# High parts first in grouped products, decay products moved ahead, in a two-block language model kernel

## The reference, cut to what matters

```python
# block 1, once a layer
h = rms_norm(x, norm1_g[l]) * (1 + sc1) + sh1
p = h @ w_in[l]
...
state = (state * w_t[:, :, None, :] - sk[..., None] * (a_t * kk_t)[:, :, None, :]
         + v_t[..., None] * k_t[:, :, None, :])            # one step of the recurrence
...
h2 = rms_norm(x, norm2_g[l]) * (1 + sc2) + sh2
x = x + gt2 * ((silu(gate) * up) @ w_down[l])
# block 2, once a layer
u = rms_norm_2(h, g_mix_pre)
gq, gk, gv, gg, ra_f, ra_b, ... = split(u @ w_in)
la_f = log_sigmoid(ra_f @ w_alpha_up[0] + b_alpha[0]) / 16   # decays of the four heads, and la_b
q_dec = q * exp(cum); k_intra = k * exp(-cum)                # cum: running sum of la in a chunk
...
h = h + rms_norm_2((silu(gate) * up) @ w_ffn_out, g_ffn_post)
h = h + rms_norm_2(sigmoid(h @ w_ple_gate) * e, g_ple_post)
```

## Time and profile before

| what | value |
|---|---|
| median of 3 runs | 3910.09 us (3908.43 to 3912.69) |
| profiled execution | 3911.07 us |
| its span, first to last instruction | 3909.2 us |
| TensorE, VectorE, ScalarE, GpSimd busy | 95%, 46%, 22%, 58% |
| mean granted TensorE clock | 0.975 |
| TensorE's share of the chain that ended last | 86% |
| weight chunks | 1082 of 256 KB |

### The profile page before, as it was taken

The page is one execution under the profiler, slowest core; times in us unless marked ns, Lnnn a source line. Parts: engine busy times, 40 slices in busy tenths (PEclk is TensorE's granted clock), DMA queues, the critical chain, the costliest instruction groups (busy, mean ns, idle before and its releaser), DMA issues.

```text
span 3909.2 us, 52952 instructions
## 1 busy us (share of the span) xinstructions
PE 3731.4 (95%) x21300; PEld 3022.7 (77%) x21300; DVE 1806.1 (46%) x2338; ACT 851.7 (22%) x1334; POOL 2274.0 (58%) x2218
## 2 busy tenths in 40 slices
PE   5999999999999899999899999999989999999997
PEld 4777678887777678887788677888777876778886
DVE  5643754234744653124443654523454435553235
ACT  3322110004222110003321532000243225220002
POOL 4512768776512767774556356777645463567773
PEclk9999999999999999998999999999989999999999
DMA  4223444342223443332223133333312231323332
GB/s 184 87 83 103 138 143 146 113 151 77 75 82 99 137 146 108 97 97 66 75 73 122 52 102 82 97 97 96 98 50 79 86 103 55 110 82 97 97 97 68
DMA packets 192195, 386.08 MB, mean 99 GB/s; under 512 B 21456, under 2 KB 21584, under 8 KB 190288
## 3 DMA queue, kind: packets, MB, share of 16 engines
q1 hardware_dynamic: 169776, 338.24, 29.1%
q10 hardware_dynamic: 22176, 44.45, 3.2%
HBM read 361.64 MB, written 20.97 MB: 98 GB/s over the span
## 4 chain that ended last, share of the span: by engine, by line
PE 86%; DVE 8%; ACT 4%; DMA 1%; issue 1%; ACTq 0%; SPq 0%; DVEq 0%
PE psum L420 18%; PE psum L421 18%; PE psum L422 18%; PE psum L492 3%; PE psum L494 3%; PE psum L493 3%; PE psum L514 2%; PE psum L981 1%; PE psum L956 1%; PE psum L599 1%; PE psum L611 1%; PE psum L467 1%; PE psum L468 1%; PE psum L469 1%; PE psum L618 1%; PE psum L572 1%
## 5 line engine op out<-in xcount | busy, mean ns | idle before, releaser
L2245 POOL TENSOR_SCALAR w_hi<-raw 128x512 fp32r<-128x512 f32 x1082 | 747.3, 691 | 1493.2 <-DMA raw<-weight_chunks 1489.5
L2247 POOL TENSOR_TENSOR w_lo<-raw,w_hi 128x512 fp32r<-128x512 f32 x1082 | 1491.1, 1378 | 90.3
L420 PE MATMUL psum<-in_hi,w_hi 128*128 128x512 f32 x1920 | 761.6, 397 | 3.8 <-ACT hs L1325 1.3
L421 PE MATMUL psum<-in_lo,w_hi 128*128 128x512 f32 x1920 | 749.3, 390 | 0.0
L422 PE MATMUL psum<-in_hi,w_lo 128*128 128x512 f32 x1920 | 748.8, 390 | 0.0
L420 PEld LDWEIGHTS psum<-in_hi,w_hi 128*128 128x128 f32 x1920 | 361.8, 188 | 91.7 <-issue 11.1
L421 PEld LDWEIGHTS psum<-in_lo,w_hi 128*128 128x128 f32 x1920 | 361.7, 188 | 79.8 <-issue 6.2
L422 PEld LDWEIGHTS psum<-in_hi,w_lo 128*128 128x128 f32 x1920 | 361.6, 188 | 75.7
L492 PE MATMUL psum<-in_hi,w_hi 128*128 128x512 f32 x576 | 255.0, 443 | 0.0
L494 PE MATMUL psum<-in_hi,w_lo 128*128 128x512 f32 x576 | 226.5, 393 | 0.0
L493 PE MATMUL psum<-in_lo,w_hi 128*128 128x512 f32 x576 | 226.4, 393 | 0.0
(11 more groups left out here) (427 smaller groups left out, 6700.4 us busy)
## 6 DMA issues: line engine op xcount, KB each, us to landing
raw<-weight_chunks SPq DMA_DIRECT2D x1082, 256.0 KB, 2.6
ada_col<-ada_slabs SPq DMA_DIRECT2D x80, 512.0 KB, 4.3
spill<-gate_st ACTq DMA_DIRECT2D x56, 256.0 KB, 2.7
ada_at<-ada_slabs SPq DMA_DIRECT2D x8, 1024.0 KB, 15.6
gin<-spill ACTq DMA_DIRECT2D x32, 256.0 KB, 3.4
mgs<-spill ACTq DMA_DIRECT2D x32, 256.0 KB, 3.0
sml<-small ACTq DMA_DIRECT2D x4, 1024.0 KB, 5.2
spill<-nt ACTq DMA_DIRECT2D x16, 256.0 KB, 2.6
```

The source lines that it names most:

```text
L420: pe.matmul(bank[:], wh, hi[:, i, :], start=(i == 0), stop=False)
L421: pe.matmul(bank[:], wh, lo[:, i, :], start=False, stop=False)
L2245: ts(w_hi[:, slot, :], raw[:, slot, :], 1.0, 1.0, ALU.mult, ALU.mult).then_inc(sem("chunk_hi"), 1)
L2247: ins = tt(w_lo[:, slot, :], raw[:, slot, :], w_hi[:, slot, :].bitcast(F32), ALU.subtract)
```

## The change

1. `late_group` and `group` become one function, `stepped`. For each tile it waits for `hi_ready`, issues for every member the two matmuls with the high part (high weight, low weight), then waits for `split_ready` and issues for every member the matmul with the low part. A chunk is given back, and in the last tile a member is finished, by its low matmul. In the six-member groups the spread of the root stands between the two passes of the last tile instead of in its middle.
2. GLA: decay 2 goes ahead of head 1's queries and keys, decay 3 ahead of head 1's values (both were one place later: 2 ahead of and 3 behind the values). The first two heads' projections rotate over three PSUM banks; the change to two comes behind them.
3. `FILL_SCORE` (0, 2, 2, 4) to (0, 2, 0, 5), `FILL_MEAN` (16, 12) to (16, 13), `FILL_CORE` (8, 2, 2, 8) to (5, 2, 2, 15).
4. The multiplication of the recurrence's state goes from the end of a chunk into the next one, between VectorE's masks for levels 1 and 2.
5. The last square ahead of the `m5` norm goes ahead of the load of the root's table.

```diff
-FILL_SCORE = (0, 2, 2, 4)
-FILL_MEAN = (16, 12)
+FILL_SCORE = (0, 2, 0, 5)
+FILL_MEAN = (16, 13)
...
-FILL_CORE = (8, 2, 2, 8)
+FILL_CORE = (5, 2, 2, 15)
...
+            def stepped(members, key, pools, order, norm=None):
+
+                banks = []
                 for k in range(DT):
+                    if norm and k == DT - 1:
+                        norm_tokens(norm)
+                    pe.wait_ge(sem("hi_ready"), count("hi_ready", (key, k)))
+                    parts = []
+                    for n, (name, matrix, l, m) in enumerate(members):
+                        if k == 0:
+                            banks.append(begin(name, pools[n], order))
                         wh, wl = next_block((matrix, l, k, m))
+                        pe.matmul(banks[n][:], wh, in_hi[:, k, :], start=(k == 0), stop=False)
+                        pe.matmul(banks[n][:], wl, in_hi[:, k, :], start=False, stop=False)
+                        parts.append((wh, cursor["chunk"], cursor["at"] == CHUNK))
+                    if norm and k == DT - 1:
+                        norm_spread(norm)
+                    pe.wait_ge(sem("split_ready"), count("split_ready", key + (k,)))
+                    seen.add(("split_ready", key + (k,)))
+                    for (name, _, _, _), bank, (wh, chunk, last) in zip(members, banks, parts):
+                        ins = pe.matmul(bank[:], wh, in_lo[:, k, :], start=False, stop=(k == DT - 1))
                         if k == DT - 1:
+                            touched.add(chunk)
                             ins.then_inc(done_sem(name), 1)
                             close(name)
+                        elif last:
                             ins.then_inc(sem("chunk_left"), 1)
+                            touched.remove(chunk)
+                            chunk_end[chunk] = sem("chunk_left"), passed("chunk_left")
...
                 side_jobs([(("g2a", l, m), "w_in2", l, N_GA + m) for m in range(DT)], "bg2")
+                gla_in(l, 0, h_in, 0, 1)
+                gla_decay(l, 2)
+                gla_in(l, 1, h_in, 3)
                 lane[0] = "lin2"
-                gla_in(l, 0, h_in, (0, 1))
-                gla_in(l, 1, h_in, (2, 3))
...
                     if m:
                         square_gated(l, m - 1)
+                square_gated(l, DT - 1)
                 af(warm[:], eps[:, 2:3], ACT.Sqrt).then_inc(sem("scalar_step"), 1)
                 act.wait_ge(sem("scalar_step"), passed("scalar_step"))
-                square_gated(l, DT - 1)
                 norm_root(("m5", l))
...
                 level_part(1)
+                if c:
+                    ins = tt(st[:], st[:], sscal[:, :, c - 1:c].to_broadcast([P, RT, P]), ALU.mult)
+                    ins.then_inc(sem("state_ready"), 1)
+                    dve.wait_ge(sem("state_ready"), passed("state_ready", (l, c)))
                 level_part(2)
...
-                    ins = tt(st[:], st[:], sscal[:, :, c:c + 1].to_broadcast([P, RT, P]), ALU.mult)
-                    ins.then_inc(sem("state_ready"), 1)
-                    dve.wait_ge(sem("state_ready"), passed("state_ready", (l, c + 1)))
```

More of the change, by code:

```diff
@@ L477, in _, with late_group, group @@
+                            touched.remove(chunk)
+                            chunk_end[chunk] = sem("chunk_left"), passed("chunk_left")
+            def late_group(l, members, pools):
+                stepped(members, ("m3", l), pools, "late", ("m3", l))
+            def group(members, key):
+                stepped(members, key, ("lin",) * len(members), "lin")
             side = {"jobs": [], "at": 0, "bank": None, "pool": None}
@@ L696, in block1 @@
                 norm_sum(("n1", l), parts=(l == 0))
-                group([(("p", l, m), "w_in", l, m) for m in (M_WA, M_GL, M_GLV)], h_in)
+                group([(("p", l, m), "w_in", l, m) for m in (M_WA, M_GL, M_GLV)], ("n1", l))
                 projection(("p", l, M_K), "w_in", l, M_K, h_in)
@@ L820, in token_major, with gla_in @@
                     close(name + (t,))
-            def gla_in(l, h, h_in, decays=()):
+            def gla_in(l, h, h_in, first=None, second=None):
                 if h:
@@ L825, in gla_in @@
                     projection(("gk", l, h), "w_in2", l, N_GK + h, h_in)
-                for d in decays[:-1]:
-                    gla_decay(l, d)
+                if first is not None:
+                    gla_decay(l, first)
                 token_major(("gv", l, h), l, "w_in2", N_GV + 2 * h)
-                for d in decays[-1:]:
-                    gla_decay(l, d)
+                if second is not None:
+                    gla_decay(l, second)
                 for j in range(2):
@@ L1015, in block2 @@
                 h_pl = lambda i: ("split_ready", ("pl", l, i))
-                group([(("pg", l, m), "w_ple_gate", l, m) for m in range(3)], h_pl)
+                group([(("pg", l, m), "w_ple_gate", l, m) for m in range(3)], ("pl", l))
                 for m in range(3, DT):
@@ L1334, in _, with gla_in @@
             squares(("m1", 0), ("rs", ("nf", 0)))
-            def gla_in(l, h, decays=()):
+            def gla_in(l, h, first=None, second=None):
                 if h >= 2:
@@ L1448, in block2 @@
                 act.wait_ge(bank_read(job), turn(job))
[L1449 to L1450 removed]
+                gla_in(l, 0, 0, 1)
+                gla_decay(l, 2)
+                gla_in(l, 1, 3)
                 gla_factors(l, 0)
```

41 lines of the change are left out of this document (2 added, 39 removed).

## The result

Four runs of the changed kernel have a median of **3857.65 us** (3852.76 to 3862.01), four of the kernel before 3909.53 us. The ratio is 0.9866, with a 95% interval of 0.9853 to 0.988: 52 us less, where 37 were forecast. Faster was right; the time lies 3.4 us under the lower end of the range.

A forecast was written before the change was run, and what follows sets the result against it. TensorE, in flight for 95% of the span, was taken as the bound, so only idle time and lower-clock time could be won. Terms summed to 37.4 us off 3911.07 (3873.7); with the median 1.0 lower, forecast 3873, range 3861 to 3889.

The forecast's parts named there:

- GLA (20.7): Attention's decays, both layers: 5.7 us at the value products, 11.4 before head 0, 3.6 at and behind head 3.
- Rival C: Attention: decays move but the wait before head 0 does not, ScalarE becoming the bound; 11.4 us less gain, 3884; chance 0.11.
- B: Rival: `qd` and `kd` run at short durations and all four clock stretches go; 5.2 + 3.4 us more, 3864; chance 0.15.
- the groups (4.1): Ten grouped products: earlier starts, partly lost to later banks; nothing for `n1`/`n2`, 0.6 `m1`, 2.3 `m3`, 1.2 us `pl`.
- Rival A: Grouped products: the new order keeps its whole gain, the bank being free in time; 7.2 us more, 3866; chance 0.10.
- the last norm (3.2): Last `m5` norm: square first, table load beside TensorE's sums, root earlier; 1.6 us each, 3.2 us.
- the recurrence (7.7): Block 1's eight chunks: earlier `mt` chain minus put-off fill steps; 4.1 us in layer 1, 3.6 in layer 0.
- the clock (1.7): Stretches at the lower clock level: two gone (3.4 us), one new behind the heads (1.7); 1.7 us net.
- So 1.2 per chunk: Recurrence: without VectorE's 1.24 us pause the chain starts about 1.2 us earlier in each chunk, 9.6 us before put-off fill.
- I take two stretches as gone: Behind the `mt` waits: waits shrink to about 1.6 us and two of four lower-clock stretches go, 3.4 us.
- E, slower: the clock: Rival: less fill makes TensorE fall to the lower clock more often, mean below 0.965, time past 3918; chance 0.03.
- D: Rival, recurrence: put-off fill costs what earlier `mt` gives, no clock stretch goes; 7.7 + 3.4 us less gain, 3884; chance 0.11.

The follow-up runs named there:

- q_square: The kernel before with only the last square moved ahead of the root's table load: 3907.08 us over ten runs, ratio 0.9998.
- before: The kernel before the change, nothing edited: median 3909.53 us over four runs.
- after: The kernel with the whole change: median 3857.65 us over four runs, ratio 0.9866 to the kernel before.
- f_score: The kernel before with FILL_SCORE (0, 2, 0, 5) and FILL_MEAN (16, 13) alone, state product not moved: 3883.78 us, ratio 0.9938.
- f_count: The kernel before with FILL_SCORE (0, 2, 2, 3) and FILL_MEAN (16, 13): 3900.67 us over ten runs, ratio 0.9973.

## Why the prediction was right and wrong

**Right: GLA (20.7).** It measured 19.7 alone. The chain held: factors behind the last gate evacuation (8.99 us from there to TensorE, 9.13 forecast), the value products' waits gone, the wait at head 3 gone and the new wait at 2.79 and 2.47 us. The wait before head 0 is 4.65 us, under the 5.5 to 6.5 named as the sign, because 0.75 us of waiting moved ahead of the fill steps, which now wait for the last gate's bank (`PE psum L485 <- ACT sg L1354`). Rival C is out. So is the half of B that hoped for short `qd` and `kd`: the last product still takes 1.63 us.

**Right: the groups (4.1).** They measured 4.1 alone, with an interval of 2 to 10, so the agreement to the tenth is luck. The start is 0.85 earlier (0.84 forecast), and behind the group stands a wait of 1.04, in the range of 0.9 to 1.5 that the prediction gave. Rival A is out.

**Too large: the last norm (3.2).** By the rows 1.4. The failed step is "behind the product at 2833.90": that time came from a product of 0.69 us, and with the change the product of layer 0 ran beside a split and took 1.62 (1.75 in the changed kernel). In layer 1 the sums ran at the higher level already in the kernel before, so there was less to hide the load behind. No drain behind a table load shows: in layer 1 the warm-up ends and the root starts 0.05 us later, 1.55 us after the load began. The loss is not the one that the Trainium skill, page "ScalarE: Activation LUTs", section "What ACT_TABLE_LOAD costs", would give.

**Wrong: the recurrence (7.7) and the clock (1.7).** For the fill constants alone the prediction has 7.7 and two clock stretches, 11.1 us; they measured 25. These 14 us are as much as the error of the whole forecast. The pause of VectorE went as forecast, 1.20 us a chunk, and the state product was hidden as forecast. The first step that failed is "So 1.2 per chunk": the chain behind the scores was moved by 1.2 us with its durations kept. These held operations of 0.99 and 1.64 us whose own length is 0.69, and the prediction named the cause of just such a stretch, for `kd`, two parts further up. The change moves two fill steps; a fill step uses up a weight block, a used-up chunk starts a fetch and a split, so the split moved too. That gives 1.25 us in chunk 0 and in four others, and 8.3 us over the eight, since three chunks are still touched.

The second step that failed is "I take two stretches as gone", 1.7 us net. In the profiled execution the clock gave 19 us of busy time. All four stretches at the `mt` waits went, by the prediction's 1.7 each 6.8 us; the other 12 us lie elsewhere, and no run isolates what ended those stretches. What the traces show is the place at the `mt` waits: of the 112 waits in the fourteen kernels, none of the 66 of up to 1.57 us is followed by a stretch at the lower level, and 29 of the 46 of 1.73 us or more are. The forecast expected 1.6 us and priced half of the stretches as staying; the waits came out at 0.75 to 1.50.

In the sum of idle time the surplus is hidden. The `mt` waits fell by 9.0 us where about 4 was forecast (2.1 to 1.6, eight times), so all other terms together fell short by some 6 us, the norm by 1.8 of it. "E, slower: the clock" was on the wrong side: the mean rose to 0.982. Rival B had the clock half right (all four stretches go) but its other half, the short `qd` and `kd`, was wrong; and at 3864 it, too, was too slow.

**D** is out: fill alone gives 25 us. The put-off steps cost more than was written at one place. The wait for the last gate in layer 0 grew from 3.18 to 5.49 us, and 1.2 of that was forecast.

**The range.** It was built from the forecast's own terms and had no end for a gain in VectorE's durations outside GLA, nor for a clock that improves by more than the four stretches. One row would have given it: the last `mt` operation of 1.64 us with its wait of 2.1. Taken at 0.69, with the first ones, it is 1.25 us in up to eight chunks, 10 us more, and 3863 as the other end of this term; 8.3 came.

The Trainium skill, page "SBUF — State Buffer", section "Who interferes with whom", has VectorE and GpSimd share one pair of ports. The traces agree on which operations are hit: the masks with one input in PSUM stay near 0.72 us each beside a split (four in 2.87 us), while products of two SBUF inputs go from 0.69 to 1.6. The Trainium skill has it there as an exclusive lock, and the rows agree: an operation of VectorE that is hit ends 0.53 to 0.55 us after the GpSimd instruction beside it has ended. In the kernel before, `w_lo` ends at 178.05 and the last `mt` operation at 178.60. In `q_square` the `w_lo` that began at 2836.73 took 1.27 us, not stretched, and ended at 2838.00; the product of `yy` that it held up ended at 2838.55. All 173 stretched operations that write `mt`, `bm`, `kd` or `yy` in five of the traces (`before`, `after`, `f_score`, `f_count`, `q_square`) do so. The other way round, the subtraction at 176.47 in the kernel before, which begins while such an operation runs, takes 1.58 us, where the one at 167.13 takes 1.27. So the one that comes second waits, and the length of a hit operation can be worked out from where the split ends.

## What to carry to other kernels

When a change moves work that uses up a shared supply (weights here), ask what the supply's next refill will run beside: a duration in the trace that is longer than the same operation's elsewhere is a term of the sum, with its short value as the other end. Three changed filler constants gave 25 us and the rewrite of ten groups 4, in part because they set what GpSimd does during three short VectorE operations. And a wait that is won at one place, as behind the groups, is only won if the granted clock and the next chain leave it: read idle time and busy time of the bound engine apart, with the count of its instructions beside them.

## What of the hardware was unexpected

- The same 21300 matmuls were in flight for 3731.4 us in one kernel and 3707.2 in the other, at a mean granted clock of 0.975 and 0.982. Idle time fell by 34.2 us beside it, and some 19 of the 24.2 us of busy time are the clock.
- GpSimd's subtractions stretch VectorE's time by 323 us of 1806 (18%), and the operations seen to be hit have both inputs in SBUF. Each of those looked at ends 0.53 to 0.55 us after the split instruction that held it up.
- No `mt` wait of up to 1.57 us was followed by a stretch at the lower clock level (66 waits), 29 of 46 longer ones were.
- One fill step fewer ahead of the chunk products, with the order kept, moved the splits from the last `mt` operation to the first pair in some chunks and off all of them in others, and gave 8.5 us.
